# A hybrid decoder layer with x scaled in place and transposed, weights and parameters packed ahead, and a bias row spread inside memory

## What is computed

```
xn = rms_norm(x, mix_norm_g)                       # x * rsqrt(mean(x^2) + eps) * g
proj = einsum('bsd,de->bse', xn, w_in)             # 2048 -> 5504
q_a, k_a, v_a, u_s5, q_h, f_h, i_h, g_h = split(proj)
attn = diff_attention(q_a, k_a, v_a, rel_bias, ...)  # 6 heads, bias by distance from a 32-bucket table
s5   = s5_mixer(u_s5, ...)                         # complex diagonal state space, 640 channels, GLU
hg   = hgrn2_mixer(q_h, f_h, i_h, g_h, ...)        # gated linear recurrence, 5 heads
h = x + concat(attn, s5, hg) @ w_out
h = h + hier_moe(rms_norm(h, ffn_norm_g), ...)     # 32 experts, 2 for each token
out = rms_norm(h, final_norm_g)
```

## Time and profile before

| what | before |
|---|---|
| median of 3 runs | 2212.87 us (2212.49 to 2216.74) |
| the profiled execution, first to last instruction | 2209.1 us |
| PE busy | 1838.8 us, 83% |
| DVE busy | 426.9 us, 19% |
| ACT busy | 256.8 us, 12% |
| POOL busy | 161.8 us, 7% |
| bytes moved, mean rate | 525.00 MB, 238 GB/s |
| the chain that ended last | PE 56%, DMA 37%, DVE 3% |

### The profile page before, as it was taken

How to read it: one execution, slowest core, us unless ns; L and a number is a source line. 1 busy time by engine, 2 the same in 40 slices (tenths; PEclk the granted TensorE clock), 3 DMA queues, 4 the chain that set the end, 5 groups by cost and what they waited for, 6 DMA issues and landing times.

```text
span 2209.1 us, 30075 instructions
## 1 busy us (share of the span) xinstructions
PE 1838.8 (83%) x13111; PEld 1073.7 (49%) x13111; DVE 426.9 (19%) x973; ACT 256.8 (12%) x602; POOL 161.8 (7%) x206
## 2 busy tenths in 40 slices
PE   7959999999999999999829777777877787787871
PEld 6425489966668568999713222222222222222220
DVE  3211332326425222000251000000000000000005
ACT  2001111110134223101200000000000000000002
POOL 2313323000000000000010000000000000000000
PEclk9979999999999999999959998998999989899995
DMA  6432333231122142222249999999999999999986
GB/s 175 101 83 76 92 78 92 57 99 51 45 58 72 50 146 56 65 72 77 96 205 422 425 422 422 413 424 412 405 416 397 422 400 424 414 416 423 413 338 252
DMA packets 185726, 525.00 MB, mean 238 GB/s; under 512 B 20374, under 2 KB 144458, under 8 KB 147440
## 3 DMA queue, kind: packets, MB, share of 16 engines
q1 hardware_dynamic: 164640, 493.44, 57.3%
q0 software_dynamic: 8976, 24.49, 3.6%
q10 hardware_dynamic: 11968, 4.89, 1.0%
HBM read 510.42 MB, written 29.75 MB: 245 GB/s over the span
## 4 chain that ended last, share of the span: by engine, by line
PE 56%; DMA 37%; DVE 3%; ACT 1%; another core or an unknown queue 1%; issue 1%; SPq 1%; POOLq 0%; DVEq 0%; POOL 0%; ACTq 0%
PE psum L673 20%; PE psum L687 18%; DMA arena<-in_moe_w_gate 12%; DMA arena<-in_moe_w_down 11%; DMA arena<-in_moe_w_up 11%; PE psum L900 7%; PE psum L917 3%; PE psum L779 2%; PE psum L712 1%; DVE arena L1181 1%; PE psum L810 1%; PE psum L838 1%; DMA arena<-expert_rows 1%; PE psum L823 1%
## 5 line engine op out<-in xcount | busy, mean ns | idle before, releaser
L900 PE MATMUL psum<-arena 128*32 128x512 f32 x4096 | 509.5, 648 | 171.9 <-DMA arena<-in_moe_w_gate 63.1
L673 PE MATMUL psum<-arena 128*128 128x128 f32 x3968 | 452.5, 276 | 0.0
L673 PEld LDWEIGHTS psum<-arena 128*128 128x128 f32 x3968 | 449.0, 193 | 2.2 <-issue 1.7
L687 PE MATMUL psum<-arena 128*128 128x512 f32 x914 | 404.2, 599 | 26.6 <-DMA arena<-in_w_in 23.0
L900 PEld LDWEIGHTS psum<-arena 128*32 128x32 f32 x4096 | 160.3, 118 | 520.6 <-issue 520.6
L687 PEld LDWEIGHTS psum<-arena 128*128 128x128 f32 x914 | 172.6, 192 | 233.1 <-issue 232.7
L917 PE MATMUL psum<-arena 128*32 128x512 f32 x2048 | 229.8, 601 | 48.4 <-DMA arena<-in_moe_w_down 48.2
L917 PEld LDWEIGHTS psum<-arena 128*32 128x32 f32 x2048 | 71.8, 111 | 194.8 <-issue 194.7
L1181 DVE TENSOR_TENSOR arena<-arena 128x128 f32<-128x128 f32 (+15 forms) x395 | 141.7, 404 | 22.5 <-ACT arena L971 14.3
L1181 DVE TENSOR_TENSOR arena<-arena,psum 128x512 f32<-128x512 f32 (+2 forms) x21 | 12.0, 574 | 672.0 <-PE psum L900 671.9
L971 ACT ACTIVATE arena<-psum 128x512 f32<-128x512 f32 (+4 forms) x118 | 60.6, 536 | 510.5 <-PE psum L687 262.1
(11 more groups left out here) (187 smaller groups left out, 891.3 us busy)
## 6 DMA issues: line engine op xcount, KB each, us to landing
arena<-in_moe_w_gate SPq DMA_DIRECT2D x64, 2048.0 KB, 28.9
arena<-in_moe_w_up SPq DMA_DIRECT2D x64, 2048.0 KB, 33.5
arena<-in_moe_w_down SPq DMA_DIRECT2D x64, 2048.0 KB, 28.3
arena<-in_w_in SPq DMA_DIRECT2D x43, 1024.0 KB, 6.1
arena<-in_w_out SPq DMA_DIRECT2D x16, 1024.0 KB, 7.0
arena<-in_x SPq DMA_DIRECT2D x8, 1024.0 KB, 10.5
arena<-expert_rows SPq DMA_DIRECT2D x8, 1024.0 KB, 13.6
hs_rows<-arena SPq DMA_DIRECT2D x4, 1024.0 KB, 4.6
```

The source lines that it names most:

```text
L673: last = mm(B(bank, [(1, P)], off=quarter * P), F(lhs + k * S + quarter * P, P), F(slot + k * P, P), start=(k == 0), stop=(k == KD - 1))
L687: last = mm(B(bank, [(1, S)]), F(slot + k * P, P), F(rhs + k * S, S), start=(k == 0), stop=(k == n - 1))
L900: last = mm(B(bank, [(1, FE)], 32 * g, 32), F(XT + c * CAP + 32 * g, 32), F(SLOT[slot] + (c % 8) * FE, FE), start=(c == 0), stop=(c == KD ...
```

## The change

It has four parts.

1. x is scaled in place by DVE (128x2048, one for each tile) instead of the 128x128 identity, and PE transposes with the plain identity, in transpose form. The semaphore `x_diag` becomes `x_scaled`.
2. The host packs `w_in`, `w_out` and `s5_w_glu` into chunks, so that a chunk is one contiguous run for each partition (8 KB in place of 16 runs of 512 bytes). It also packs the S5 b and c arrays, and puts the norm weights, five small vectors and the router weights into one array, `params`.
3. ACT now loads only the identity. The rest of the constants and `params` are issued on SP's queue, behind the four tiles of x and ahead of the first chunks of `w_in`. DVE waits for both (`consts_in`) ahead of its first copy of a transposed bank.
4. The six bias rows are stored once (15 KB, `b_d`). After its first tables POOL issues six DMAs from DRAM to DRAM that write each row 128 times.

```diff
@@ sync
             for t in range(TB):
                 sp.dma_start(F(H0 + t * D, D), DV(d["x"], t * P * D, [(D, P), (1, D)])).then_inc(x_in[t], 16)
+            sp.dma_start(F(GMIX, NPK), DV(d["params"], 0, [(NPK, P), (1, NPK)])).then_inc(consts_in, 16)
+            sp.dma_start(F(CON + P, ncon - P), DV(d["consts"], P, [(ncon, P), (1, ncon - P)])).then_inc(consts_in, 16)
...
-                sp.dma_start(V(RING[i % NW], [(P, rows), (1, P)]), src).then_inc(chunk_in[i % NW], 16)
+                sp.dma_start(F(RING[i % NW], rows * P),
+                             DV(src, at_ * P * rows * P, [(rows * P, P), (1, rows * P)])).then_inc(chunk_in[i % NW], 16)
@@ gpsimd
-            for i, name in enumerate(("s5_c_re", "s5_c_im")):
-                for half in range(2):
-                    pool.dma_start(V(CNAT + i * 640 + half * SN, [(P, 5), (1, SN)]),
-                                   DV(d[name], 0, [(SN, P), (P * SN, 5), (1, SN)])).then_inc(cnat_in, 16)
+            pool.dma_start(F(CNAT, 1280), DV(d["s5_c"], 0, [(1280, P), (1, 1280)])).then_inc(cnat_in, 16)
             for dst, src in [
-                (V(BRAW, [(SC, NQ), (1, SC)]), DV(d["s5_b_re"], 0, [(SC, P), (P * SC, NQ), (1, SC)])),
-                (V(BRAW + 320, [(SC, NQ), (1, SC)]), DV(d["s5_b_im"], 0, [(SC, P), (P * SC, NQ), (1, SC)])),
-                (V(WR, [(36, KD), (1, 4)]), DV(d["moe_w_group"], 0, [(KD * 4, P), (4, KD), (1, 4)])),
-                (V(WR + 4, [(36, KD), (1, 32)]), DV(d["moe_w_router"], 0, [(KD * 32, P), (32, KD), (1, 32)])),
...
+                (F(BRAW, 640), DV(d["s5_b"], 0, [(640, P), (1, 640)])),
...
             pool.wait_ge(bias_row, 1)
-            pool.dma_start(DV(r_d, 0, [(P * RB, AH), (RB, P), (1, RB)]),
-                           V(RR, [(0, P), (1, RB)], 0, AH)).then_inc(bias_out, 16)
+            pool.dma_start(DV(b_d, 0, [(RB, AH), (1, RB)]), F(RR, RB, 0, AH)).then_inc(bias_out, 16)
...
             w1(0)
             ca(0)
+            pool.wait_ge(bias_out, 16)
+            for h in range(AH):
+                pool.dma_start(DV(r_d, h * P * RB, [(RB, P), (1, RB)]),
+                               DV(b_d, h * RB, [(0, P), (1, RB)])).then_inc(bias_spread, 16)
...
-            pool.wait_ge(bias_out, 16)
+            pool.wait_ge(bias_spread, 16 * AH)
@@ tensor
-                    once(x_diag, t + 1)
+                    once(ident_in, 16)
+                    once(x_scaled, t + 1)
                     for c in range(4):
-                        last = mm(B(bank, [(1, P)], off=c * P), V(H0 + t * D + 4 * q + c, [(KD, P)]),
-                                  F(DIAG + t * P, P), start=True, stop=True)
+                        last = tr(B(bank, [(1, P)], off=c * P), V(H0 + t * D + 4 * q + c, [(KD, P)]), ident)
@@ scalar
-            act.dma_start(F(CON, ncon), d["consts"]).then_inc(consts_in, 16)
-            act.dma_start(F(GMIX, KD), DV(d["mix_norm_g"], 0, [(KD, P), (1, KD)])).then_inc(consts_in, 16)
+            act.dma_start(F(CON, P), DV(d["consts"], 0, [(ncon, P), (1, P)])).then_inc(ident_in, 16)
...
+            act.wait_ge(consts_in, 32)
@@ vector
                         settle(v.reciprocal(F(RST + t1, 1), F(STD + t1, 1)))
-                        if t1 == 0:
-                            dve.wait_ge(consts_in, 32)
-                        ts(F(DIAG + t1 * P, P), F(IDENT, P), F(RST + t1, 1), None, M).then_inc(x_diag, 1)
+                        ts(F(H0 + t1 * D, D), F(H0 + t1 * D, D), F(RST + t1, 1), None, M).then_inc(x_scaled, 1)
+                    if (t, q) == (0, 0):
+                        dve.wait_ge(consts_in, 32)
```

More of the change, by code:

```diff
@@ L121, in build @@
         IDENT = C["ident"]
+        GMIX = take(KD)
+        LBL, D5, SUB, HNG = take(HH), take(NB5), take(1), take(1)
         WR = take(KD * 36)
-        GMIX = take(KD)
-        LBL, LBE, LBR, LB, LB1, D5 = take(HH), take(HH), take(HH), take(HH), take(HH), take(NB5)
-        SUB, SUBG, HNG = take(1), take(1), take(1)
+        LBE, LBR, LB, LB1 = take(HH), take(HH), take(HH), take(HH)
+        SUBG = take(1)
         LAMD, LAME, NLAM = take(2), take(2), take(1)
@@ L138, in build @@
         GIDX, SIDX = [take(1), take(1)], take(1)
+        NPK = KD + 2 * HH + 2 + KD * 36
+        assert WR + KD * 36 - GMIX == NPK
         H0 = 2600
@@ L211, in build @@
         y_d = scratch("y_scratch", [NB5 * P, S])
+        b_d = scratch("bias_row", [AH, RB])
         r_d = scratch("bias_rows", [AH * P, RB])
@@ L402, in chunk @@
                 if kind == "glu":
-                    rows, src = 5, DV(d["s5_w_glu"], j * P, [(640, P), (P * 640, 5), (1, P)])
+                    rows, src, at_ = 5, d["s5_w_glu"], j
                 elif kind == "wo":
-                    rows, src = KD, DV(d["w_out"], j * P, [(D, P), (P * D, KD), (1, P)])
+                    rows, src, at_ = KD, d["w_out"], j
                 else:
-                    rows, src = KD, DV(d["w_in"], COLS[kind] + j * P, [(KD * NIN, P), (NIN, KD), (1, P)])
-                sp.dma_start(V(RING[i % NW], [(P, rows), (1, P)]), src).then_inc(chunk_in[i % NW], 16)
+                    rows, src, at_ = KD, d["w_in"], COLS[kind] // P + j
+                sp.dma_start(F(RING[i % NW], rows * P),
+                             DV(src, at_ * P * rows * P, [(rows * P, P), (1, rows * P)])).then_inc(chunk_in[i % NW], 16)
             def part(e, place, which, half):
@@ L718, in do @@
                 elif kind == "cT":
-                    once(cnat_in, 64)
+                    once(cnat_in, 16)
                     tiles = [(s[1], t) for t in range(4)] if s[1] < 2 else [(0, 4), (1, 4)]
@@ L723, in do @@
                 elif kind == "rb":
-                    once(params_in, 16 * 12)
+                    once(params_in, 16 * 5)
                     last = mm(B(bank, [(1, 320)], 0, AH), F(RELB, AH, 0, 32), F(OH + s[1] * 320, 320, 0, 32),
@@ L834, in do @@
                 elif kind == "rt":
+                    once(consts_in, 32)
                     for q in range(16):
@@ L1696, in _, with chunks_of, columns_of @@
                                        M).then_inc(out_ready, 1)
-_IN = ["x", "w_in", "w_out", "mix_norm_g", "ffn_norm_g", "rel_bias", "diff_lambda", "attn_subln_g", "s5_a_re",
-       "s5_a_im", "s5_log_dt", "s5_b_re", "s5_b_im", "s5_c_re", "s5_c_im", "s5_d", "s5_w_glu", "hgrn_lb_logits",
-       "hgrn_norm_g", "moe_w_group", "moe_w_router", "moe_w_gate", "moe_w_up", "moe_w_down", "final_norm_g"]
+_IN = ["x", "ffn_norm_g", "rel_bias", "diff_lambda", "s5_a_re", "s5_a_im", "s5_log_dt", "moe_w_gate", "moe_w_up",
+       "moe_w_down", "final_norm_g"]
+def chunks_of(w, rows_first):
+    k = w.shape[0] // P
+    a = w.reshape(k, P, -1, P).transpose(2, 1, 0, 3) if rows_first else w.reshape(P, k, -1, P).transpose(2, 0, 1, 3)
+    return np.ascontiguousarray(a).reshape(-1, P, k * P)
+def columns_of(v, n):
+    return np.ascontiguousarray(v.reshape(n, P).T)
 def arrays_of(inputs):
@@ L1707, in arrays_of @@
     arrays = {}
+    whole = {}
+    for name in inputs:
+        a = np.ascontiguousarray(inputs[name])
+        whole[name] = a[0] if a.ndim > 1 and a.shape[0] == 1 else a
     for name in _IN:
-        a = np.ascontiguousarray(inputs[name])
-        arrays[name] = a[0] if a.ndim > 1 and a.shape[0] == 1 else a
+        arrays[name] = whole[name]
+    arrays["w_in"] = chunks_of(whole["w_in"], False)
+    arrays["w_out"] = chunks_of(whole["w_out"], True)
+    arrays["s5_w_glu"] = chunks_of(whole["s5_w_glu"], True)
+    arrays["s5_b"] = np.concatenate([whole[n].reshape(NQ, P, SC).transpose(1, 0, 2).reshape(P, NQ * SC)
+                                     for n in ("s5_b_re", "s5_b_im")], axis=1)
+    arrays["s5_c"] = np.concatenate([np.repeat(whole[n].reshape(NB5, P, 1, SN).transpose(1, 0, 2, 3), 2,
+                                               axis=2).reshape(P, NB5 * P) for n in ("s5_c_re", "s5_c_im")], axis=1)
+    router = np.concatenate([whole["moe_w_group"].reshape(P, KD, NGRP), whole["moe_w_router"].reshape(P, KD, NE)],
+                            axis=2).reshape(P, KD * 36)
+    arrays["params"] = np.ascontiguousarray(np.concatenate([
+        whole["mix_norm_g"].reshape(P, KD), columns_of(whole["hgrn_lb_logits"], HH), columns_of(whole["s5_d"], NB5),
+        columns_of(whole["attn_subln_g"], 1), columns_of(whole["hgrn_norm_g"], 1), router], axis=1))
     arrays.update(consts=block, onehot=onehot, masked=masked)
```

9 lines of the change are left out of this document (3 added, 6 removed).

## The result

The changed kernel takes 2178.7 us (median, 2175.7 to 2181.12, 4 runs) against 2212.68 before (4 runs): a ratio of 0.984, 95% interval 0.9819 to 0.9861, 34 us less. The forecast was 2180.4, range 2171 to 2194. The profiled execution spans 2178.9 us against 2209.1.

A forecast was written before the change was run, and what follows sets the result against it. PE bounds the first half up to about 1161 us, expert weight DMA the rest, which stays. 2209.1 - 25.2 (hole) - 7.3 (transposing steps) = 2176.6 us of span, plus 3.8 to the median: 2180.4, range 2171 to 2194.

The forecast's parts named there:

- The hole: PE's 22.89 us wait from 114.35 for a `w_in` chunk, plus slow clock after it; forecast to go entirely, -25.2 us.
- rival 5: The bias row was only a companion of PE's wait for `w_in`, so that wait stays: 2205.6 us, chance 0.03.
- slow end of the spread: Bound on the bias row's spread: 16 engines at 9.8 GB/s each, 157 GB/s, 1.97 MB in 12.6 us.
- Rival 1: The bias spread is as slow as the old store and PE's wait only moves: 2203 us, chance 0.06 whole or in part.
- Packed chunks: zero: Packing `w_in` and `w_out` may land chunks faster than 6.1 us, but PE needs 13.8 for one: no gain.
- 25 us of cover: `UP` loads queue behind the spread on POOL; PE wants them at about 124, so their delay is hidden by 25 us.
- The transposing steps: The 16 steps at the start: DVE limits instead of PE, first projection at 34.7 against 42.49; sum -7.3 us.
- The 0.5 for a slow clock during the steps: PE idles some 6 us after tile 0's transposes, its clock falls, a few steps take 0.85 instead of 0.74: +0.5 us.
- the ends I gave: Range for the start's gain, -10.5 to -3 us; constants landing at 15.2 (412 GB/s) or 22.6 us (310 GB/s).
- rival 2: The clock stays low under transposes; first eight projection matmuls cost 5.58 instead of 3.44, +2.1: 2184 us, chance 0.06.
- my signs of being wrong: A hole after about 107 us released by `UP` or `w_in`; clock 0.50 at first projection; expert stage not 999 us.

The follow-up runs named there:

- e1: The kernel before with only the bias row's new form (stored once, spread by six DRAM to DRAM DMAs after POOL's first tables): 2188.23 us, ratio 0.9888.
- e3: The changed kernel with each bias row written 128 times straight from its SBUF partition, by six DMAs in the old store's place: 2214.11 us, one run.
- e6: The changed kernel with the spread as one DRAM to DRAM DMA of the old shape instead of six DMAs: 2178.72 us, ratio 0.984.
- e7: The changed kernel with `w_in` and `w_out` unpacked, chunks in runs of 512 bytes again: 2181.58 us.
- e2: The changed kernel with the old store of the bias row (one DMA from six SBUF partitions, 1920 KB): 2190.74 us, ratio 0.9915.
- e10: The kernel before with `w_in` and `w_out` packed into contiguous chunks and nothing else: 2199.6 us, ratio 0.9937.
- e11: The changed kernel again, unchanged, run beside the second run of the version that loads the norm weights first: 2177.57 us.
- e8: The changed kernel again, unchanged, as comparison for other variants of its set: 2176.84 us.
- e9: Second run of the changed kernel with the norm weights loaded alone and first, DVE's first copy waiting only for them: 2174.88 us.
- e4: The changed kernel with the norm weights loaded alone and first, DVE's first copy waiting only for them: 2173.45 us, ratio 0.9829.

## Why the prediction was right, step by step

**The hole, -25.2.** Right in place and size: -25.1 in e1, and in the changed kernel the quarters at 143.84 come at 112.47, 31.37 earlier, of which the start gives 6.2 and the hole 25.2. The cause was right too: e1 changes nothing but the bias row's spread and the hole is gone, which answers rival 5. Two steps under it were wrong without moving the sum. The slow end of the spread, "each engine no faster than the 9.8 GB/s above, on 16 engines 157 GB/s", took the 9.8 for a property of the engines. It was the source: with nearly all 16 engines on one partition of SBUF the rate was 26 GB/s for all together (e3), with six engines on DRAM it was 26 GB/s for each (e6). The row that carried the forecast was the other one, `ffn_norm_g`, a load that reads one row of DRAM 128 times. The spread took 10.0 us, where I took 12. Rival 1 feared the writes, and e6 clears them; a form with 16 engines that is as slow as the old store does exist, though, with SBUF as its source: it is e3. And "Packed chunks: zero" holds only with the store gone (e7). Beside the store, packing removes the whole wait for `w_in` (e2, e10).

**The wait that stood behind.** I found `UP` behind the spread in POOL's queue and gave it 25 us of cover; that held, as it landed at 96.0 and was wanted at 123. I did not see that beside the old store it was late as well, inside the hole; e2 and e10 bring it out with 8.9 and 9.8 us.

**The transposing steps, -7.3.** The start came 7.9 us earlier (34.60 against 42.49), and the clock took 1.7 of it back in the profiled execution, which leaves 6.2. The mechanism was right, PE no longer the limit and DVE behind the constants in its place, but that the size came out so near is luck: four terms were off, and they nearly cancel. The constants landed at 20.6, not 18.3 (+2.3). By then 6.98 MB had moved, not 6.5, and 5.68 MB of it over SP's queue, where x, parameters and constants make 5.2: some of `w_in` had passed before the constants were all in. That it passed on engines that were done sooner is an inference. The rate, 367 GB/s from 1.6 us on, was below my 390 as well. The copies have a pitch of 0.60 us, not 0.74 (2.39 for four), so DVE needed 13.9 us and not 16.2 (-2.3). The scaling took 1.29 us, 1.23 interpolated. The 0.5 for a slow clock during the steps was not needed (-0.5), since DVE did not wait for PE behind the constants; the clock's price came later, in the first chunk (+1.7). In the ends I gave, the early one was itself worked out wrong: 5.3 MB at 412 GB/s from 1.6 us on is 14.5, not 15.2.

**The clock, rival 2.** The Trainium skill (TensorE: Matmul & The Clock Gate, Part 4) says that transposes do not count as PE activity in the same way, so that the full clock is not reached under them. That is not what the runs show: in the changed kernel the clock stands at 0.50 from 20 to 22 and at 1.00 from 28 to 30 with nothing but transposes between, and in e7 and e11 it never fell in the waiting at all up to 28. But the rival's price, 2.1 us and a little more in the first chunk, is close to the 1.7 that some executions pay after 34 us, and one of my signs of being wrong, a clock of 0.50 at the first projection, did come, in 2 of 7 profiles. That the sparse transposing steps before it bring the dip about is an inference; no run here changed their density alone.

**The rest.** The first expert matmul comes 32.9 us earlier, 1128.55 against 1161.44; in e8 and e11, the same program, it comes at 1126.68 and 1131.60, so 5 us of scatter lie ahead of it, more than separates the forecast from the median. The expert stage takes 2.7 us longer from the first expert matmul to the last copy (1128.55 to 2130.13 against 1161.44 to 2160.37), in the single execution of each. That it depends on addresses wasn't tried. From the first expert matmul to the end e8 takes 1047.7 us, the first profile of the changed kernel 1050.3 and the kernel before 1047.6, so two executions of one program differ by as much. The 1.7 us between forecast and median say nothing more of the terms.

## What to carry to other kernels

Here a DMA that copies one row many times was priced by its source before its shape (58.9 us against 20.4, then 10.0): read the row out of DRAM, not out of the SBUF partition that happens to hold it, and then give it an outer dimension that all engines share. Where a load has to pass such a slow transfer, few long runs pass it sooner than many short ones. When a wait is removed, look for what else stands in the slow transfer's own queue: a second wait of some 9 us came out from behind the first one here. And where a small operand gates the first instruction of a chain, load it alone and first; bundled with 1 MB of constants behind x it came 7 us later than needed.

## What the runs showed of the hardware that I had not expected

- A DMA source of one SBUF partition gave 26 GB/s over nearly all 16 engines, 1.7 GB/s each (e3); six partitions 57 GB/s over six engines, not six times as much; one row of DRAM for each of six engines 26 GB/s an engine (e6).
- Beside that store, a 1 MB load landed in 50.3 us as 2048 packets and in 25.6 to 25.9 us as 128 (e2, e10), at the same total size. The long packets were expected to bring it to 10.
- TensorE's clock fell to 0.50 within 1.5 us of the start of back-to-back matmuls, behind transposes with pauses, in 2 of 7 profiles of one and the same start; it was back at 1.00 from 38 us on in one (e11) and from 40 in the other. It fell so once in two profiles of the version with an earlier start (e9, not e4).
